# Two feed-forward layers of a float32 block: first weights and gate rows issued one block of code earlier, up halves signalled apart, and the last K step of a weight stream run job by job

## The reference, cut to what matters

```
def dwconv3(t, w, b):
    tp = jnp.pad(t, ((0, 0), (1, 1), (0, 0)))
    return tp[:, :-2] * w[0] + tp[:, 1:-1] * w[1] + tp[:, 2:] * w[2] + b

def conv_ffn(h, w_up, cw, cb, w_down):
    u = dwconv3(h @ w_up, cw, cb)
    a, b = jnp.split(u, 2, axis=-1)
    return (jax.nn.silu(a) * b) @ w_down

for layer in range(2):
    ...                                     # mixer: u = modulate(rmsnorm(x)) @ w_in, ..., w_out
    h = modulate(rmsnorm(x, norm_ffn_g[layer]), sh2, sc2)
    x = x + g2 * conv_ffn(h, ffn_w_up[layer], ffn_conv_w[layer], ffn_conv_b[layer], ffn_w_down[layer])
    if layer == 0: ...                      # the same for the 256 context tokens
```

## Time and profile before

| | |
|---|---|
| runs, median (lowest to highest) | 4101.6 us (4098.0 to 4104.9) |
| the profiled execution, its own time | 4096.7 us |
| its span, first to last instruction | 4094.9 us |
| TensorE busy | 3481.8 us (85%) |
| VectorE busy | 2587.3 us (63%) |
| ScalarE busy | 2228.4 us (54%) |
| mean granted TensorE clock | 0.909 of 2.4 GHz |
| up, layer 0 and layer 1 | about 2555 to 2922 and 3677 to 3919 us |
| down, layer 0 and layer 1 | about 2943 to 3138 and 3935 to 4073 us |

### The profile page before, as it was taken

The page is one execution under the profiler, slowest core; times in us unless marked ns, Lnnn a source line. Parts: engine busy times, 40 slices in busy tenths (PEclk is TensorE's granted clock), DMA queues, the critical chain, the costliest instruction groups (busy, mean ns, idle before and its releaser), DMA issues. The chain is left out here.

```text
span 4094.9 us, 51212 instructions
## 1 busy us (share of the span) xinstructions
PE 3481.8 (85%) x17582; PEld 2847.8 (70%) x17582; DVE 2587.3 (63%) x3511; ACT 2228.4 (54%) x2850; POOL 583.5 (14%) x284
## 2 busy tenths in 40 slices
PE   7879999847979999767988986999897988869987
PEld 6757777646757777545887765888675877558865
DVE  4659999855569999786456555444344565545545
ACT  2549998833449999785344552333233444634433
POOL 0005333400005334400002220000000002300000
PEclk9979999968979999977998878999898999779998
DMA  3049999821049999894110011111121220022222
GB/s 106 27 147 415 419 419 412 345 102 38 19 163 417 419 417 415 325 395 172 57 48 32 1 34 40 62 61 61 57 62 41 71 67 2 1 68 93 101 76 79
DMA packets 139776, 643.21 MB, mean 157 GB/s; under 512 B 22110, under 2 KB 35808, under 8 KB 76000
## 3 DMA queue, kind: packets, MB, share of 16 engines
q1 hardware_dynamic: 129116, 622.92, 39.5%
q0 software_dynamic: 10080, 16.80, 1.1%
q10 hardware_dynamic: 432, 1.57, 0.1%
HBM read 636.77 MB, written 24.36 MB: 161 GB/s over the span
## 5 line engine op out<-in xcount | busy, mean ns | idle before, releaser
L1533 DVE TENSOR_TENSOR w_low<-w_raw,w_high 128x2048 fp32r<-128x2048 f32 x392 | 881.3, 2283 | 63.0 <-ACT w_high L1530 58.1
L1530 ACT CAST w_high<-w_raw 128x2048 fp32r<-128x2048 f32 x392 | 745.9, 1910 | 86.7 <-DMA w_raw<-in_moe_down_dram 41.0
L1840 PE MATMUL banks<-w_high,x_split 128*128 128x512 f32 x1024 | 421.2, 411 | 44.4 <-DVE w_low L1533 37.2
L1840 PE MATMUL banks<-w_low,x_split 128*128 128x512 f32 x1024 | 407.8, 398 | 0.0
L446 PE MATMUL banks<-w_high,x_high 128*128 128x512 f32 (+2 forms) x808 | 310.7, 385 | 68.4 <-DVE w_low L367 43.4
L334 ACT CAST w_high<-w_raw 128x512 fp32r<-128x512 f32 (+2 forms) x200 | 117.8, 589 | 447.2 <-PE banks L446 420.1
L3131 PE MATMUL banks<-x_high,w_high 128*128 128x512 f32 (+1 forms) x1056 | 318.4, 355 | 35.6 <-DVE w_low L3171 35.6
L3131 PE MATMUL banks<-x_low,w_high 128*128 128x512 f32 (+1 forms) x1056 | 317.6, 355 | 0.0
L3131 PE MATMUL banks<-x_high,w_low 128*128 128x512 f32 (+1 forms) x1056 | 317.3, 354 | 0.0
L446 PE MATMUL banks<-w_low,x_high 128*128 128x512 f32 (+2 forms) x808 | 302.4, 374 | 0.0
L446 PE MATMUL banks<-w_high,x_low 128*128 128x512 f32 (+2 forms) x808 | 302.4, 374 | 0.0
(11 more groups left out here) (411 smaller groups left out, 7563.5 us busy)
## 6 DMA issues: line engine op xcount, KB each, us to landing
w_raw<-in_moe_gate_dram SPq DMA_DIRECT2D x132, 1024.0 KB, 11.0
w_raw<-in_moe_up_dram SPq DMA_DIRECT2D x132, 1024.0 KB, 10.2
w_raw<-in_moe_down_dram SPq DMA_DIRECT2D x132, 1024.0 KB, 10.9
w_raw<-in_w_ada_dram SPq DMA_DIRECT2D x48, 1024.0 KB, 12.4
w_raw<-in_ffn_w_up_dram SPq DMA_DIRECT2D x44, 1024.0 KB, 4.8
w_raw<-in_ffn_w_down_dram SPq DMA_DIRECT2D x88, 256.0 KB, 2.7
w_raw<-in_w_cols_dram SPq DMA_DIRECT2D x48, 256.0 KB, 2.7
w_raw<-in_w_out_dram SPq DMA_DIRECT2D x32, 256.0 KB, 3.0
```

What stands on the lines that cost most here:

```text
L1530: act.copy(ex["WS"][0][:, v % HIGH, :], ex["WR"][:, v % RAW, :]).then_inc(ex["high"], 1)
L1533: dve.tensor_tensor(ex["WS"][1][:, v % LOW, :], ex["WR"][:, v % RAW, :], ex["WS"][0][:, v % HIGH, :].bitcast(F32), ALU.subtract).then_inc( ...
L1840: ins_ = pe.matmul(GU[b][m], stationary(b, kk), WS[w][:, s, k * BANK:(k + 1) * BANK], start=(kk == 0 and w == 0), stop=(kk == KD - 1 and w ...
```

## The change

It has four parts.

- **First up weights.** The 1 MB transfer of up tile 0 is issued by SP in the norm block, behind the `gain` load. The norm's transposed output goes to the first eight rows of `hiddenT`, so that `w_raw` has room. SP's loop in `ffn_up` starts at tile 1.
- **First down weights and gate rows.** After the low part of the last up tile, SP issues inside the up block the weights of the first peeled row tiles of down (2, since `peeled(22)` is 2) and the gate rows. These go to the buffer that held the up weights. The block `gates` with its barrier is gone; VectorE waits for the gate rows (`loaded`) at its first leave. `stream` skips the two transfers.
- **Up halves.** TensorE adds 1 to `multiplied` after each half; ScalarE waits for half a before it copies a and for half b before it copies b.
- **Last column block of any `stream`.** In row tile K-2 TensorE does only the first half of the jobs. In tile K-1 it goes through the jobs one by one: for a job of the second half the products of tile K-2 and then those of K-1, for one of the first half those of K-1; after each it adds 1 to `last_done`, and each job's leave waits for its own count. This holds for `down0`, `down1`, `u0` and `u1`.

```
-    def stream(self, name, X, K, blocks, convolution=None):
+    def stream(self, name, X, K, blocks, convolution=None, ahead=None):
...
+                    if ahead and c == 0 and isinstance(k, int) and k < peeled:
+                        return
                     sp.wait_ge(low, n + 1)
...
-                    dve.wait_ge(used, (c + 1) * K + S)
+                    if c == len(blocks) - 1:
+                        dve.wait_ge(last_done, g - first_job[c] + 1)
+                    else:
+                        dve.wait_ge(used, (c + 1) * K + S)
...
+                        if g == 0 and ahead:
+                            dve.wait_ge(ahead["loaded"], ahead["loads"])
...
+                    late = js[len(js) // 2:]
+                    if c == len(blocks) - 1 and isinstance(k, int) and k == K - 2:
+                        for g in js[:len(js) // 2]:
+                            products(g, rest, False)
+                        return
+                    if c == len(blocks) - 1 and stop:
+                        for g in js:
+                            if g in late:
+                                products(g, rest - 1, False)
+                            products(g, rest, True).then_inc(last_done, 1)
+                        return
...
+    def first_tiles(self, ahead, block, K, loads=()):
+
+        def issue(sp):
+            for k in range(min(4, self.peeled(K))):
+                sp.dma_start(ahead["W"][:, k, 0:block[1]], block[0][:, k * block[1]:(k + 1) * block[1]]).then_inc(
+                    ahead["raw_in"][k], 16)
+            for dst, src in loads:
+                sp.dma_start(dst, src).then_inc(ahead["loaded"], 16)
+        return issue
...
+                def first_unit(sp):
+                    sp.dma_start(W[:, :], ins["ffn_w_up"][layer * NF]).then_inc(raw_in, 16)
...
-                    tiles(sp, tile)
+
+                    with sp.Fori(0, NF // 2 - 1) as i:
+                        for b in range(2):
+                            load(i * 2 + (1 + b))
+                    load(NF - 1)
+                    sp.wait_ge(low, NF + 1)
+                    following(sp)
...
-                    pe.sem_inc(multiplied, 2)
+                    pe.sem_inc(multiplied, 4)
...
-                        ins_.then_inc(multiplied, 1)
+                            ins_.then_inc(multiplied, 1)
...
-                        act.wait_ge(multiplied, f + 3)
                         act.wait_ge(left, f + 1)
                         for ab in range(2):
+                            act.wait_ge(multiplied, f * 2 + (ab + 5))
```

More of the change, by code:

```diff
@@ L435, in tile, with products @@
                 def tile(c, k, n, rest, turns):
-                    by_weights, js = blocks[c][2], range(first_job[c], first_job[c + 1])
-                    pe.wait_ge(low, n + (1 + R))
+                    js = range(first_job[c], first_job[c + 1])
                     start = isinstance(k, int) and k == 0
                     stop = isinstance(k, int) and k == K - 1
-                    for g in js:
-                        if start and g >= banks:
-                            pe.wait_ge(out_a if by_act[g - banks] else out_v, turn[g - banks] + 1)
+                    def products(g, rest, stop):
+                        by_weights = blocks[c][2]
                         _, (a, b), (x, y), _, _ = jobs[g]
@@ L447, in tile @@
                                              start=start and first + second == 0, stop=stop and first == 1)
+                        return ins_
+                    pe.wait_ge(low, n + (1 + R))
+                    late = js[len(js) // 2:]
[9 more added lines that the diff above has]
+                        return
+                    for g in js:
+                        if start and g >= banks:
+                            pe.wait_ge(out_a if by_act[g - banks] else out_v, turn[g - banks] + 1)
+                        ins_ = products(g, rest, stop)
                     ins_.then_inc(used, 1)
@@ L2380, in modulation, with modulated @@
             self.end(sem)
-    def modulated(self, name, layer, which, XT, tiles, beside=None, XS=None):
+    def modulated(self, name, layer, which, XT, tiles, beside=None, XS=None, issue=None):
         nc, ins = self.nc, self.ins
@@ L2401, in modulated @@
                                   for t in range(tiles)], "rms", RMS_EPS,
-                           [(gain[:, :], ins[("norm_mix_g", "norm_ffn_g")[which]][layer])], None, None, turn, beside)
+                           [(gain[:, :], ins[("norm_mix_g", "norm_ffn_g")[which]][layer])], None, None, turn, beside, issue)
     def token_rows_of(self, t):
         return self.H[:, t, :] if t < NT else self.C[:, t - NT, :]
[L2408 to L2413, removed]
     def gate_rows(self, ctx, layer, part, vectors):
```

54 lines of the change are left out of this document (31 added, 23 removed).

## The result

The changed kernel takes 4067.9 us (median of four runs, 4067.7 to 4076.1), beside 4099.8 us for the kernel before (four runs, 4093.8 to 4104.9): a ratio of 0.9921, 95% interval 0.9908 to 0.9933. The forecast was 4069 with 4060 to 4080. The profiled execution took 4067.8 us, its span is 4066.0, its mean granted clock 0.913 (0.909 before).

The account below looks back on a forecast made before the run. TensorE was taken to bound up and down inside, with idle gaps between blocks and VectorE alone at down's end. 7.9 + 3.7 + 15.6 + 6.3 - 0.9 = 32.6 us; 4101.6 - 32.6 = 4069, range 4060 to 4080.

Parts of the forecast that it names:

- Entry of up: Start of up: first cast waits for the taps, no longer the 1 MB transfer; 4.2 and 3.7 us gained, sum 7.9.
- Up halves: Tail of up's last tile: VectorE starts on b where it started on a; 2.2 and 1.45 us gained, sum 3.7.
- rival (c): Layer 1's up loop: added rows lengthen ScalarE's chain, making the kernel slower, 4110 us; chance 0.02.
- From up to down: Gap between up and down: only one barrier and the split remain; 8.6 and 7.0 us gained, sum 15.6.
- Rival (a): Entry of down: late because three engines must fetch new code at once; 4077 or 4085 us; chance 0.12.
- the half case: Entry of down: code fetch takes half the removed block's time; the 15.6 us term falls to 7.8, time 4077.
- End of the streams: Stream ends: leaves start sooner in down, 4.2 and 2.1 us gained; projections lose 0.45 us twice.
- Clock: Starts after the gaps: both should start at the low level as now, so the clock adds no term.
- rival (b): Starts leave the low clock sooner, or the shorter gap before down1 no longer drops it; 4063 us; chance 0.11.
- the allowance of 1 us per start: Time at the low clock: allowed to vary 1 us either way for each of four starts.
- One of the criteria: Anywhere untouched: the forecast is wrong if a stage the change does not touch moves by more than 2 us.

Follow-up runs that it names:

- filling: Changed kernel plus matmuls and transposes with unused results that keep TensorE at work in the gap before down: 4061.2 us, ratio 0.9898.
- both small edits: Changed kernel with ScalarE waiting for the taps behind its first cast and only gated streams ending job by job: 4067.4 us.

## Why the prediction was right

**Entry of up.** The late part was the taps, as the step said; moving their wait gave the further 1.7 us per layer that the step had put at 1.8. The early transfer didn't delay `gain`: from its issue to the last `x_low` of the norm layer 0 took 27.43 us before and after, layer 1 19.21 and 19.18.

**Up halves.** Both tails by their own terms; layer 1's loop did not lengthen, so rival (c) is out.

**From up to down.** The barrier was costed from the nearest row at 0.98 us and took 0.88 and 0.89; the split at 3.0 and 2.5 took 3.00 and 2.52. Rival (a) is false: ScalarE entered `stream` straight from up's block with no delay beside that of any barrier, and what VectorE and TensorE needed lay inside the split, which took what it took before. Nor did the queues of kind "instruction", which the profile lists beside the data queues, move anything then. The DMA view from 2920 to 2931 us has one queue:

```profile
q1 hardware_dynamic: 302, 0.55, 17.3%
```

By the Trainium skill (Runtime: NRT & Kernel Launch, Instruction fetch mechanics) a taken branch to a page not held must wait for its fetch; nothing here shows such a wait at this entry, and 0.88 us leaves no room for the 3.9 us per layer of the half case.

**End of the streams.** First leave 1.07 us after the last low part was ready (1.0 forecast), six leaves without a pause, 4.1 and 2.05 us. The loss in the projections was 0.5 and 0.6 where 0.45 was forecast; the sign was right, and so an edit that should have been limited to gated leaves cost 1.1 us.

**Clock.** The 9.13 and 7.18 us gaps both still started low, so rival (b) is out; down 1 did come off the low clock 1.3 us sooner than before, worth 0.5 us. But the allowance of 1 us per start was too small. Over twelve profiles without filling, TensorE stayed low at the start of down 0 for 2.7 to 6.1 us (4.4 before, 5.7 after), and in down 1 for 4.0 to 6.1 (5.7 before, 4.4 after). And the prediction took TensorE to be the bound throughout down, which it isn't: when the first column block ends, TensorE waits 2.0 us in down 0 and 2.8 us in down 1 for `w_low`, before and after alike, and in most profiles the clock then drops a second time.

**The 3.2 us between the stage sum (32.1) and the profiled difference (28.9)** come from stages that the table leaves out. Down's streams took 0.9 and 0.6 us more after. In down 0 the first 60 matmuls account for 0.6 of it, and the rest follows behind the middle. In down 1 the start gained those 0.5 us, and the part behind the middle lost 1.1, since the clock stood at 0.50 there for 6.8 us instead of 3.4. The code ahead of the first norm took 2.06 us more and layer 0's projections up to their last `w_low` 2.1 less, where the clock stood at 0.50 for 17.1 us after the first 12 us and for 23.9 before; the change touches neither. The remaining differences are each under 1 us and add up to 1.7.

So the forecast of 32.6 us stood within half a microsecond of the stages by each term. That the time came out within about 1 us of it (4067.9 where 4069 was forecast) is in part luck: the median of the kernel before was 4101.6 us in three runs and 4099.8 in four, and between 4099.6 and 4106.7 beside the experiments. One of the criteria, that no untouched stage moves by more than 2 us, was badly chosen: the start of the first norm lies between 1902.2 and 1907.5 in the profiles of kernels that are the same up to there.

## What to carry to other kernels

Where blocks are separated by barriers, list per boundary what the first engine of the next block waits for, and issue that transfer in the block ahead; a block that only loads costs its barriers and its landing, 5.9 and 4.3 us here. When one wait is removed, read off what is late next (here the taps) and move it in the same edit. Ending a stream job by job pays where the leaves are long beside the job's matmuls (1.45 against 0.7 us), and costs where they are shorter and shared. And where single runs scatter by 10 us, a gain of 1 to 5 us is read in its stage, from the rows at its two ends, not in the total. Even in its stage, look at the granted clock all the way through before a microsecond is put down to an edit.

## What the runs showed of the hardware that was not expected

**Two rates of the same loop at the same clock.** Layer 0's up, with its pairs of 512 and 256 columns, took 373.4 to 374.0 us from first matmul to the end of `hiddenT` in eight of fourteen profiles and 380.4 to 381.1 in the other six (375.2 and 382.7 in the two with the longer tail), at granted clock 1.00 and without idle time in both. Windows of the changed kernel and of the one with one count for both halves (PE count in brackets):

```profile
2600.00:2650.00 50.00, 50.00 (x290) 44.09 (x289) 23.65 (x31) 17.87 (x15) 0.00 (x0) 1.00 0.20 74
```

```profile
2600.00:2650.00 50.00, 50.00 (x285) 43.37 (x284) 23.39 (x31) 17.53 (x15) 0.00 (x0) 1.00 0.17 63
```

Pairs in the timeline, first of the changed kernel, then of the other:

```profile
2701.00 0.51 PE L3178 MATMUL banks<-x_high,w_high 128*128 128x512 f32 x2
2701.34 0.51 PE L3178 MATMUL banks<-x_low,w_high 128*128 128x512 f32 x2
2701.69 0.51 PE L3178 MATMUL banks<-x_high,w_low 128*128 128x512 f32 x2
2702.04 0.51 PE L3178 MATMUL banks<-x_high,w_high 128*128 128x512 f32 x2
```

```profile
2700.93 0.53 PE L3178 MATMUL banks<-x_high,w_high 128*128 128x512 f32 x2
2701.29 0.51 PE L3178 MATMUL banks<-x_low,w_high 128*128 128x512 f32 x2
2701.64 0.51 PE L3178 MATMUL banks<-x_high,w_low 128*128 128x512 f32 x2
2701.99 0.53 PE L3178 MATMUL banks<-x_high,w_high 128*128 128x512 f32 x2
```

Three pairs take 1.04 us in the one and 1.06 in the other, 0.53 instead of 0.51 us for one pair in three. The stage has 352 such sets of three, so 0.02 us each gives the 7 us. The pattern is there from the first pairs after the clock has risen and stays for the whole stage. Layer 1's up, without pairs, stays within 1.1 us (244.9 to 246.0; 246.9 and 247.1 with the longer tail). Kernels on either side differ only in parts that don't touch the pairs, and the repeated kernel's times form two groups about 6 us apart, so it may be drawn anew in each execution. But other stages scatter by some microseconds too, and the only kernel with two profiles shows the same rate in both, so this isn't shown, and what chooses the rate stays open.

**The stretch at the low clock varies** from 2.7 to 6.1 us between kernels with the same work at that place. It is counted here from the first matmul to the one from which they follow each other at less than 0.33 us. It isn't ordered by the length of the gap: after 9.1 us of idle time it was 5.7 in the changed kernel and 2.7 in the one with both small edits.

**A wait of 2 to 3 us inside a stage can be followed by a low stretch too.** At the change of column blocks VectorE first takes the finished jobs out of PSUM, and `w_low` comes late. TensorE's first matmul behind that wait in down 1, changed kernel:

```profile
3980.63 0.80 PE L456 MATMUL banks<-w_high,x_high 128*128 128x512 f32 x1 [2.83 <-DVE w_low L373]
```

Windows around it, then one at the same place of the kernel with both small edits, where the same wait of 2.8 us ended at 3977.37:

```profile
3975.00:3979.70 4.70, 2.80 (x12) 1.94 (x11) 4.19 (x7) 2.03 (x4) 0.00 (x0) 1.00 0.19 58
3980.00:3986.60 6.60, 5.97 (x14) 4.76 (x15) 1.78 (x3) 0.44 (x1) 0.00 (x0) 0.50 0.27 79
```

```profile
3980.00:3984.00 4.00, 4.00 (x18) 3.02 (x17) 1.29 (x2) 1.96 (x4) 0.00 (x0) 1.00 0.21 59
```

In down 1 this second low stretch lasted 6.8 us in six of the fourteen profiles, 3.4 in six, and was absent in two (both small edits, with and without filling), after a wait of 2.8 us each time. The first 150 matmuls of the second column block took 41.4 to 41.5, 40.3 to 40.5 and 38.8 to 38.9 us. In down 0, after 2.0 us, it was 6.8 us long in one profile, 3.4 in nine and absent in four. What decides between the three was not tested. No run moved the leaves off VectorE's path there, which would be the next edit to try.
